# A two-layer hybrid decoder step: gate and value of the last FFN as seven products of quarters, and B's output projection moved into A's FFN

## The reference, cut to what matters

```python
def swiglu(h, w_up, w_down):
    g, u = jnp.split(h @ w_up, 2, axis=-1)
    return (jax.nn.silu(g) * u) @ w_down

for layer in range(DEPTH):
    hn = rmsnorm(x, norm_mix[layer])
    mix, ... = mixer_even(hn, ...) if layer % 2 == 0 else mixer_odd(hn, ...)   # ends in @ w_out
    x = x + mix
    x = x + swiglu(rmsnorm(x, norm_ffn[layer]), ffn_w_up[layer], ffn_w_down[layer])
return (rmsnorm(x, norm_final), ...)        # and the mixers' states
```

## Time and profile before

| | us |
|---|---|
| three runs, median | 2490.19 (2488.18 to 2491.6) |
| profiled execution | 2490.38 |
| its span, first to last instruction | 2488.6 |
| PE busy in the span | 2434.4 (98%) |
| DVE, ACT, POOL busy | 1007.4, 870.9, 1098.4 |
| mean granted clock of PE | 0.991 |

### The profile page before, as it was taken

How to read it: one execution, slowest core, us unless ns; L and a number is a source line. 1 busy time by engine, 2 the same in 40 slices (tenths; PEclk the granted TensorE clock), 3 DMA queues, 4 the chain that set the end, 5 groups by cost and what they waited for, 6 DMA issues and landing times.

```text
span 2488.6 us, 37223 instructions
## 1 busy us (share of the span) xinstructions
PE 2434.4 (98%) x15510; PEld 2194.1 (88%) x15510; DVE 1007.4 (40%) x1712; ACT 870.9 (35%) x1155; POOL 1098.4 (44%) x605
## 2 busy tenths in 40 slices
PE   8999999899999999999999899999999999999998
PEld 6889997688887977999999889988887889999998
DVE  4513255334444435543333443344434443222224
ACT  5431135234223355443333244343432334222223
POOL 2722145555465344544354450043545544544453
PEclk9999999999999999999999999999999999999999
DMA  8863373321324477422222274432232334222222
GB/s 302 307 222 136 136 255 118 105 84 63 123 69 134 161 258 265 152 73 94 85 78 94 77 256 179 168 95 78 81 116 96 119 118 163 93 87 93 94 85 86
DMA packets 102246, 335.88 MB, mean 135 GB/s; under 512 B 12288, under 2 KB 16192, under 8 KB 102080
## 3 DMA queue, kind: packets, MB, share of 16 engines
q1 hardware_dynamic: 102080, 333.52, 39.3%
HBM read 255.20 MB, written 76.16 MB: 133 GB/s over the span
## 4 chain that ended last, share of the span: by engine, by line
PE 88%; DVE 5%; POOL 2%; issue 2%; ACT 1%; DVEq 1%; POOLq 1%; DMA 1%; SPq 0%; ACTq 0%
PE ps L807 63%; PE ps L862 18%; POOL wl L1428 1%; DMA wr<-in_wblk 1%; PE ps L902 1%; PE ps L958 1%; PE ps L956 1%; PE ps L831 0%; DVE mixl L1812 0%; ACT wh L1162 0%; DVE sq L1598 0%; POOLq L1445 0%; PE ps L1019 0%; PE ps L1016 0%; PE ps L962 0%
## 5 line engine op out<-in xcount | busy, mean ns | idle before, releaser
L1428 POOL TENSOR_TENSOR wl<-wr,wh 128x1024 fp32r<-128x1024 f32 (+1 forms) x328 | 791.5, 2427 | 553.2 <-ACT wh L1162 552.9
L807 PE MATMUL ps<-xh,wh 128*128 128x260 f32 (+2 forms) x3296 | 881.8, 322 | 6.6 <-issue 2.6
L807 PE MATMUL ps<-xl,wh 128*128 128x260 f32 (+2 forms) x3296 | 868.8, 318 | 0.0
L807 PE MATMUL ps<-xh,wl 128*128 128x260 f32 (+1 forms) x3280 | 866.8, 319 | 0.0
L807 PEld LDWEIGHTS ps<-xh,wh 128*128 128x128 f32 (+1 forms) x3296 | 543.6, 188 | 60.9 <-issue 17.9
L807 PEld LDWEIGHTS ps<-xl,wh 128*128 128x128 f32 (+1 forms) x3296 | 543.0, 187 | 44.8 <-issue 2.4
L807 PEld LDWEIGHTS ps<-xh,wl 128*128 128x128 f32 x3280 | 541.5, 188 | 44.9
L1162 ACT ACTIVATE wh<-wr 128x1024 fp32r<-128x1024 f32 (+1 forms) x332 | 342.6, 1044 | 291.3 <-DMA wr<-in_wblk 283.8
L862 PE MATMUL ps<-hidh,wh 128*128 128x260 f32 (+1 forms) x1024 | 280.8, 328 | 20.3 <-POOL wl L1428 10.3
L862 PE MATMUL ps<-hidl,wh 128*128 128x260 f32 (+1 forms) x1024 | 277.5, 324 | 0.0
L862 PE MATMUL ps<-hidh,wl 128*128 128x260 f32 (+1 forms) x1024 | 276.6, 324 | 0.0
(11 more groups left out here) (373 smaller groups left out, 2314.1 us busy)
## 6 DMA issues: line engine op xcount, KB each, us to landing
wr<-in_wblk SPq DMA_DIRECT2D x328, 512.0 KB, 3.6
split<-wh SPq DMA_DIRECT2D x64, 512.0 KB, 5.3
split<-wl SPq DMA_DIRECT2D x64, 512.0 KB, 6.3
wh<-split SPq DMA_DIRECT2D x64, 512.0 KB, 3.2
wl<-split SPq DMA_DIRECT2D x64, 512.0 KB, 4.2
xr<-in_xT SPq DMA_DIRECT2D x8, 260.0 KB, 6.3
xB<-in_xT SPq DMA_DIRECT2D x8, 260.0 KB, 6.3
out_yT<-xB SPq DMA_DIRECT2D x8, 260.0 KB, 2.2
```

The costliest lines, as they stand in the source:

```text
L807: mm = pe.matmul(ps[0:cols, b + c, 0:n], wt[:, w], xt[:, e:e + n], start=first, stop=end)
L1428: pool.tensor_tensor(lo, raw, hi.bitcast(F32), ALU.subtract).then_inc(s_lo, 1)
```

## The change

**1. Gate and value of one hidden tile of B as seven products.** Before, a tile had two units of 48 matmuls (gate and value, each over 8 inner tiles and two token pieces). Now the 2 x 2 blocks of the weights (gate or value; first or second half of the 8 inner tiles) and the 2 x 2 blocks of the activations (inner half; token half of 260) are multiplied in Winograd's form of Strassen's method: seven products (`sp`) of 4 inner tiles x 3 matmuls x 260 columns, 12 matmuls each, from sums of blocks.

- Weights: `weight_set` loads the two blocks of a tile into the first half of a set `wqr[f % 2]` (8 pieces of 512 columns); DVE forms four sums in the second half (`set_sums`: s1 = a21+a22, s3 = a11-a21, s2 = s1-a11, s4 = a12-s2); ACT rounds seven pieces in four steps (`set_hi`) and POOL subtracts in place (`set_lo`). There are two sets. The load of tile f+2 is issued after product 2 of tile f: products 0, 1, 2 are the ones that use the loaded pieces.
- Activations: DVE multiplies x by gain and norm factor (`scaled`, eight), forms four sums of 4 x 260 columns (`quarter_sum`), ACT rounds seven quarters (`quarter_hi`), DVE subtracts (`quarter_lo`). The norm is thus needed before the FFN and no longer after it. The old split of x for this norm is gone.
- Results (`products_sum`): ACT copies product 0, DVE adds the others up, seven additions of 260 columns, two of them into the halves of `hf`; ACT takes Silu of the gate and DVE multiplies by it, 520 columns. Products 2 and 4 have banks 4 and 5 for themselves, the others take turns in banks 0 to 3. POOL no longer multiplies.
- `down` weights of this FFN have slots of their own (`down_blocks`, `down_hi`, `down_lo`) outside the ring.

**2. B's output projection** stands after the `up` units of A's tenth group (g = 9) and before its `down` units. B's mixed tiles are split earlier for it, 4 to 7 first. B's quarters and the first set are prepared in what is left of A's FFN.

**3. A's final norm and output** move from `out(1, B)` into tiles 4 to 20 of the last FFN (squares at tiles 4 to 14, norm at 16, products and stores at 17 to 20).

The core of the diff:

```diff
 NORMS = ((A, "gmix0"), (B, "gmix0"), (A, "gffn0"), (A, "gmix1"), (B, "gffn0"), (B, "gmix1"), (A, "gffn1"),
-         (A, None), (B, "gffn1"), (B, None))
+         (B, "gffn1"), (A, None), (B, None))
+LAST = 7
+PIECE = (0, 1, 3, 4, 5, 6, 7)
+PSTEP = (0, 0, 1, 2, 2, 3, 3)
+PAIRS = ((0, 2), (3, 4), (4, 6), (6, 8))
...
+    def last_ffn(at):
+        for f in range(NF):
+            g, kk = f // 2, f % 2
+            for i in range(7):
+                add(("sp", f, i))
+                if i == 1 and f and (kk or f == 2):
+                    add(("hl", 1, B, (f - 1) // 2, (f - 1) % 2))
+                if i == 2 and f + 2 < NF:
+                    add(("wq", f + 2))
+                for s in at.get((f, i), ()):
+                    add(s)
+            add(("hh", 1, B, g, kk))
+            if f + 2 == NF:
+                add(("wd", NG - 1))
+            if kk and g:
+                for m in range(KT):
+                    add(("down", 1, B, g - 1, m))
+                    if m == 1:
+                        add(("hl", 1, B, g, 1))
+                    for s in at.get((f, "down", m), ()):
+                        add(s)
+                if g + 1 < NG:
+                    add(("wd", g))
...
-                           {(8, 4): [("ue", 0), ("dma", "smp1out")], (9, 0): [("ue", 1)], (9, 2): mix(1, B)[0:2],
-                            (9, 3): mix(1, B)[2:4], (9, 4): mix(1, B)[4:6], (10, 0): mix(1, B)[6:8]}))
-    out(1, B, 8, {2: [("nrm", 7), ("nrv", 7)], 3: [("fin", 0), ("fin", 1)], 4: [("fo", 0), ("fin", 2), ("fin", 3)],
-                  5: [("fo", 2), ("fin", 4), ("fin", 5)], 6: [("fo", 4), ("fin", 6), ("fin", 7)], 7: [("fo", 6)]})
-    ffn(1, B, 9, {}, halves=True)
+                          {(8, 2): mix(1, B)[4:6], (8, 4): [("ue", 0), ("dma", "smp1out")], (9, 0): [("ue", 1)] + mix(1, B)[6:8],
+                           (9, 1): mix(1, B)[0:2], (9, 2): mix(1, B)[2:4], (9, "end"): outs,
+                           (9, "down", 2): [("nrm", LAST)], (9, "down", 3): [("nrv", LAST)],
+                           (9, "down", 5): [("wS", 0)], (9, "down", 6): [("xn", 0)], (9, "down", 7): [("xn", 1), ("xn", 2)],
+                           (10, 0): [("xn", 3), ("xn", 4)], (10, 1): [("xh", 0), ("xn", 5), ("xn", 6)],
+                           (10, 2): [("xn", 7), ("xh", 1), ("xh", 5), ("xt", 0)], (10, 3): [("xt", 1), ("xh", 4), ("xt", 2)],
+                           (10, "down", 0): [("wH", 0, 0), ("xh", 3), ("xh", 2)], (10, "down", 1): [("xl", 0)],
+                           (10, "down", 2): [("wH", 0, 1), ("xh", 6)], (10, "down", 3): [("xl", 1)], (10, "down", 4): [("wH", 0, 2)],
+                           (10, "down", 5): [("xl", 2)], (10, "down", 6): [("wH", 0, 3)],
+                           (10, "down", 7): [("wq", 1), ("xl", 3)], (NG, "down", 1): [("xl", 4)], (NG, "down", 3): [("xl", 5)],
+                           (NG, "down", 5): [("xl", 6)], (NG, "down", 6): [("wS", 1)], (NG, "down", 7): [("wH", 1, 0), ("wd", 0)]}))
...
+        if f == 2:
+            places = ((1, 2), (1, 3), (1, 4), (1, 5), (2, 0))
+        elif f == 3:
+            places = ((2, 2), (2, 3), (2, 4), (2, 5), (2, 6))
+        elif f % 2:
+            places = ((f - 2, "down", 6), (f - 1, 0), (f - 1, 1), (f - 1, 2), (f - 1, 4))
+        else:
+            places = ((f - 1, 3), (f - 1, 4), (f - 1, 5), (f - 1, "down", 1), (f - 1, "down", 4))
+        for n, p in enumerate(places):
+            put(p[0], p[1:], ("wH", f, n - 1) if n else ("wS", f))
+    for g in range(NG):
+        first, second = ((3, 0), (3, 2)) if g == 0 else ((2 * g + 2, 5), (2 * g + 3, 0)) if g < NG - 1 else ((NF - 1, 3), (NF - 1, 5))
+        put(first[0], first[1:], ("wD", g, 0))
+        put(second[0], second[1:], ("wD", g, 1))
+    for m in range(KT):
+        put(4 + m + m // 2, (2,), ("xs", 8, m))
+    put(16, (0,), ("nrm", 8), ("nrv", 8))
+    for m in range(0, KT, 2):
+        put(17 + m // 2, (1,), ("fin", m))
+        put(17 + m // 2, (4,), ("fin", m + 1))
+        put(17 + m // 2, (6,), ("fo", m))
...
+            def weight_set(f):      # SP
+                if f == 0:
+                    sp.wait_ge(s_unit, pl.done(("out", 1, B, KT - 1)))
+                elif f == 1:
+                    sp.wait_ge(s_unit, pl.done(("down", 1, A, NG - 2, KT - 1)))
+                else:
+                    sp.wait_ge(s_unit, pl.done(("sp", f - 2, 2)))
...
+            def product(u, f, i):      # PE
+                pe.wait_ge(s_qhi, 4 * f + PSTEP[i] + 1)
+                pe.wait_ge(s_qlo, 4 * f + PSTEP[i] + 1)
+                if f == 0:
+                    pe.wait_ge(s_xh, KT * 7 + XQ[i] + 1)
+                    pe.wait_ge(s_xl, KT * 7 + i + 1)
+                banks_free(u)
+                b = pl.bank[u]
+                for k in range(KT // 2):
+                    w, e = slice(PIECE[i] * 512 + k * P, PIECE[i] * 512 + (k + 1) * P), slice(k * Q, (k + 1) * Q)
+                    for wt, xt, first, end in ((wqh[f % 2], xqh[i], k == 0, False), (wqh[f % 2], xql[i], False, False),
+                                               (wql[f % 2], xqh[i], False, k == KT // 2 - 1)):
+                        mm = pe.matmul(ps[:, b, 0:Q], wt[:, w], xt[:, e], start=first, stop=end)
+                mm.then_inc(s_unit, 1)
...
+            def set_lo(f, j):      # POOL
+                pool.wait_ge(s_qhi, 4 * f + j + 1)
+                pool.wait_ge(s_wsum, f + 1)
+                for n in range(*PAIRS[j]):
+                    e = slice(512 * n, 512 * n + 512)
+                    last = pool.tensor_tensor(wql[f % 2][:, e], wqr[f % 2][:, e], wqh[f % 2][:, e].bitcast(F32), ALU.subtract)
+                last.then_inc(s_qlo, 1)
...
+            def set_sums(f):      # DVE
+                a11, a12, a21, a22, s2, s1, s4, s3 = (wqr[f % 2][:, 512 * n:512 * n + 512] for n in range(8))
+                v.drain()
+                v.wait_ge(s_wq[f % 2], 32 * (f // 2 + 1))
+                v.tensor_tensor(s1, a21, a22, ALU.add)
+                v.tensor_tensor(s3, a11, a21, ALU.subtract)
+                v.drain()
+                v.tensor_tensor(s2, s1, a11, ALU.subtract)
+                v.drain()
+                v.tensor_tensor(s4, a12, s2, ALU.subtract).then_inc(s_wsum, 1)
...
+            def products_sum(it, f, i):      # DVE
+                if i in (0, 2):
+                    return
...
+                else:
+                    v.tensor_tensor(usum[:], part(6), usum[:], ALU.add).then_inc(s_evd, 1)
+                    v.drain()
+                    v.tensor_tensor(hf[:, t + Q:t + 2 * Q], part(4), usum[:], ALU.add).then_inc(s_evd, 1)
+                    v.tensor_tensor(hf[:, t:t + Q], usum[:], part(2), ALU.subtract).then_inc(s_evd, 1)
+                    v.drain()
+                    v.wait_ge(s_gsi, f + 1)
+                    v.tensor_tensor(hf[:, t:t + 2 * Q], hf[:, t:t + 2 * Q], gsum[:], ALU.mult).then_inc(s_hm, 1)
```

More of the change, by code:

```diff
@@ L84, in ffn @@
                     add(("nrm", N_FFN[L, X]))
+            for s in at.get((g, "end"), ()):
+                add(s)
             if g:
@@ L87, in ffn @@
                     add(("down", L, X, g - 1, m))
+                    for s in at.get((g, "down", m), ()):
+                        add(s)
                     if m == 1:
@@ new lines, in order, with put @@
+    at = {(0, i): [("wH", 1, j)] for i, j in ((0, 1), (2, 2), (4, 3))}
+    def put(f, step, *x):
+        at.setdefault((f, *step), []).extend(x)
+    for f in range(2, NF):
+        if f == 2:
[8 more added lines that the diff above has]
+            put(p[0], p[1:], ("wH", f, n - 1) if n else ("wS", f))
@@ L258, in order @@
+    last_ffn(at)
     return it
@@ L317, in __init__ @@
                 new = [NB * x[1] + B_FFN + (0 if g == 0 else 4 + (g - 1) * 6) + q]
[L318 to L326 removed]
+            elif k == "dh" or k == "down" and x[1:3] == (1, B):
+                continue
             elif k == "down":
@@ L997, in gla_sample_end @@
                     pe.wait_ge(s_q2, 1)
-                    pe.matmul(ps[:, 5, 64:128], ones, osq[:], start=True, stop=True).then_inc(s_qm2, 1)
+                    pe.matmul(ps[:, 5, 64:128], ones, osq[:], start=True, stop=True).then_inc(s_qm, 1)
             def mlstm_columns(X):
@@ L1101, in _ @@
                     pass
+                elif k == "sp":
+                    product(u, *v)
                 elif k == "dh":
```

312 lines of the change are left out of this document (239 added, 73 removed).

## The result

The changed kernel is slower: 2502.16 us (2498.61 to 2503.31) against 2490.19 us for the kernel before on the same chip, ratio 1.0045, 95% interval 1.0034 to 1.0057. The forecast was 2482 us, faster than before. The profiled execution took 2499.0 us with a span of 2496.8, 8.2 above the span of before; it is one of the shorter of its kernel, so the profiles lie 8 us apart where the medians lie 12 apart.

What follows compares the result with a forecast made beforehand. PE was taken as the only bound, busy 2434 of 2489 us. Terms -31.7 + 13.2 + 6 + 1.5 + 2.5 = -8.5 us took 2490.4 to 2481.9, stated as 2482 us, range 2464 to 2503.

Steps and rivals of the forecast that it cites:

- matmuls less: Last FFN: 264 fewer matmuls over 22 hidden tiles at 0.1202 us each, -31.7 us.
- projection moved, quarters prepared: Inside A's FFN: B's output projection net +1.5 us, preparing B's quarters on DVE +2.5 us.
- first two groups: Tiles 0 to 3 of the last FFN: POOL's preparation late for the first `down` unit, +6 us (0 to 12).
- eight regular groups: Tiles 4 to 19 of the last FFN: waits, squares, norm and final products, +13.2 us (0 to 28).
- 0 to 1.0 us of PE idle in a group, I take 0.8: Regular groups: PE waits at its third `down` unit for evacuations queued behind DVE's sums; 8 x 0.8 us.
- 0.6 for a square: Regular groups: each of eight squares of A delays POOL and the sums, costing 0.6 us.
- 2 for norm and final products: Tiles 16 to 20: A's last norm on ACT and final products on DVE cost 2 us in all.
- the floor: Last FFN: a two-tile group's time if only PE's matmuls count, 31.75 us, where a group took 34.63 before.
- the first groups' upper end: First two groups: 12 us as upper end of the +6 us, as a long stop can lower the clock.
- Rival 2: Regular groups: DVE's four sums each wait a whole POOL step, 4.1 us PE idle a group; 2501 us, 27%.
- 3.4 us of waits for `mixl`: Moved projection: tile 3 of B's mix ready about 27.4 us after group start, due at 24.
- The preparation of the quarters: A's last two groups: about 50 us of DVE work in 46, part of it showing, +2.5 us (0 to 10).

Runs made afterwards that it cites:

- Experiment 1: Changed kernel with the four sums of a tile's weight quarters left out, ACT copying quarters into their places; 2476.78 us, ratio 0.9950.
- 9: Changed kernel with the weight quarters' sums issued earlier and apart from tile 4 on, POOL's `down` halves earlier; 2488.45 us, ratio 0.9999.
- 11: Changed kernel with sums earlier and apart, `down` halves earlier, A's norm and final products moved, odd tiles' gate product behind the first `down` evacuation; 2481.64 us, ratio 0.9967.
- experiment 7: Changed kernel with the weight quarters' sums of even and odd tiles issued later, one by one; 2504.81 us, ratio 1.0065.
- 12: 11 with the odd tiles' sums behind `down` units 1, 3, 5, 7 in place of 2 to 5, and their roundings moved; 2504.78 us, ratio 1.0057.

## Why the prediction was wrong

The forecast's working, set against the changed kernel's profile:

| step | forecast | measured |
|---|---|---|
| matmuls less | -31.7 | -31.7 |
| projection moved, quarters prepared | +4.0 | +3.6 |
| first two groups | +6 | +7.5 |
| eight regular groups | +13.2 | +28.2 |
| behind them | 0 | +0.6 |
| sum | -8.5 | +8.2 |

Each measured term is the stretch's length after, less its length before, with 0.1202 us for each missing matmul added back.

**Right.** The rate and number of the matmuls. Place, releaser and mechanism: in the eight groups PE waits only in the second and third `down` unit, for DVE, whose evacuations stand behind sums slowed by POOL. The wait ahead of the first `down` unit of the first group, 3.60 us, has no releaser in the profile, but ends at 2143.70, where POOL's last `down` half has ended at 2143.60. No wait for a DMA. Experiment 1 prices the sums, 9 and 11 the order.

**The step that failed** is "0 to 1.0 us of PE idle in a group, I take 0.8", with 0.6 for a square and 2 for norm and final products. The eight groups were to take 13.2 us above the floor and took 28.2. By the windows: groups with one square take 34.12 to 34.27 us, the one with two at a clock of 1.00 takes 35.02. That gives about 0.85 for a square and 33.35 without one, 1.6 above the floor; norm and final products add 37.77 + 37.05 - 2 x 33.35 = 8.1. So 8 x 1.6 + 8 x 0.85 + 8.1 = 27.7 of the 28.2, as an estimate; what the clock took is within these parts. Each part was undersized:
- The square went in between POOL's steps and the sums, which ended at T + 21.4 and not 20.3. I counted 0.43 for each queued small operation, and 0.52 is what one takes with its drain. Together the first unit's bank came free 1 to 2 us later than worked out, with PE already at the end of its slack, so each delay counted in full.
- A stop was priced at its length alone. I had the row for the clock and used it for the first groups' upper end, but three regular groups had a mean clock of 0.95, about 5.5 us that no term held.
- Norm and final products were taken as 2 us in sum. They stand among the sums (a final product took 0.75 us alone before, 1.2 to 1.8 here), and experiment 4, which only moves them, took 0.2% off.

**The two prices that the Trainium skill's pages would have changed.** The fourteen products of two tiles take 20.16 us in the changed kernel, 168 matmuls at 0.120, so the row's rate held. The 110.8 ns that the Trainium skill gives for an isolated matmul (TensorE: Matmul & The Clock Gate, Back-to-back issue gap) were not reached in this stream, in which a weight load stands before every matmul. POOL's run of four `down` halves grew by some 0.97 us with two DVE operations in it, 0.48 each and not the 0.69 that full exclusion by the Trainium skill (SBUF — State Buffer, Who interferes with whom) would cost it; on DVE's side the wait shows, 1.77 us for a sum of 0.69. POOL's timeline in the changed kernel and in experiment 7, where DVE left it alone:

```profile
2204.26 5.95 POOL L1682 TENSOR_TENSOR dwl<-dwr,dwh 128x512 fp32r<-128x512 f32 x4
```

```profile
2240.96 4.98 POOL L1687 TENSOR_TENSOR dwl<-dwr,dwh 128x512 fp32r<-128x512 f32 x4
```

**Rival 2** named the time (2501), in part by luck: its price of 4.1 us a group isn't what happened. One to three of the four sums waited for POOL, mostly two, not all four; a group cost 2.4 to 6.0 us above the floor, 3.5 in the mean, and part of that was clock. The argument against it, "at t = 18 to 20 it waits for these same sums", held for the fourth sum in seven groups of eight and for the third in three.

**The moved projection** was mis-sized in part, and the sum of the transition was met by luck. I forecast 3.4 us of waits for `mixl`; PE is busy 44.60 of 44.60 us there. The preparation of the quarters was forecast at 2.5 us, and the stretch that holds it has 5.4 us of waits. PE's waits from 2000 us to the last FFN:

```profile
PE ps L1047 <- DVE xA L2136: 4.0, 4, 2.3
...
PE ps L1047 <- POOL wl L1656: 1.4, 1, 1.4
```

And the clock helped. The same 50 us ahead of the projection, before and after:

```profile
1900.00:1950.00 50.00, 50.00 (x219) 40.35 (x217) 17.17 (x40) 11.14 (x13) 27.41 (x18) 0.93 0.23 74
1900.00:1950.00 50.00, 50.00 (x237) 40.65 (x235) 22.02 (x42) 12.16 (x15) 30.54 (x18) 1.00 0.26 83
```

By an estimate, 0.07 x 50 = 3.5 us were lost to the clock before and not after. In the profiles of the changed kernel and the twelve edits the last FFN begins between 2093 and 2102 us, the median at 2099; the changed kernel's own begins at 2096.6 and that of before at 2093.0. So an estimate of what the transition costs in a usual execution is 6 us, not 3.6, and differences of a few us between two single profiles say little. No experiment separates projection and preparation. The 0.6 us behind the last group are unexplained.

## What to carry to other kernels

Where an engine that evacuates PSUM also prepares data for another engine, find for each operation both who waits behind it and who waits for it; in this kernel the same instructions in four orders (the changed kernel, 9, 11 and 12) made times from 2482 to 2505 us. When PE's slack is used up to within a microsecond, price the queue with its drains, and leave room for the clock that a stop of 2 to 3 us can cost. Work that nothing needs soon (here the product by the gate) goes behind the evacuation, not ahead of it.

## What the runs showed that was not expected

- A sum on DVE, with two SBUF inputs, takes up to 1.8 us beside a running POOL and 0.69 once POOL idles; four in a row next to POOL took 1.77, 1.77, 0.69 and 0.69 in one group and 0.75, 1.77, 1.62 and 0.69 in the next. The instruction is the same each time; what differs is what POOL does.
- Room beside each operation is not enough: with the four odd sums at every other `down` unit (experiment 12), each with room, the kernel took 23 us more than with them at every unit (11).
